# Dilated attention of a decoder layer on one Trainium2 core: both heads of a pair step together, and outputs are normalised behind the values

## What is computed

```python
h = _rms_norm(x, attn_norm_g)
z = h @ w_in                                   # q, k, v (8 heads of 64) and a, g (512 each)
q, k = _rms_norm(q, q_norm_g), _rms_norm(k, k_norm_g)
# attention: a query at t reads t, t-d, ..., t-window for (window, d) in (128,1), (512,4), (2048,16);
# the three softmaxes are combined with weights proportional to their denominators
attn, k_state, v_state = attend(q, k, v)
u = a * jax.nn.sigmoid(g)
c = silu(layer_norm(causal_depthwise(u, conv_w, conv_b)))     # 31 taps
x = x + concat([attn, c]) @ w_out
h = _rms_norm(x, ffn_norm_g)
x = x + (silu(h @ w_gate) * (h @ w_up)) @ w_down              # 2816 wide
```

## Time and profile before

| | us |
|---|---|
| Median of 3 runs | 1406.88 (1405.79 to 1413.41) |
| The profiled execution | 1401.69 |
| Its span | 1399.9 |
| Attention, first scores to first mean of the layer norm | 234.4 |
| Busy over the span: TensorE, VectorE, ScalarE, GpSimd | 1316.2, 785.7, 464.5, 540.8 |

### The profile page before, as it was taken

One profiled execution on the slowest core, in us unless ns is written; L12 is line 12 of the kernel. 1 busy time (PEld: TensorE's weight loads), 2 busy tenths in 40 slices (PEclk: granted clock), 3 DMA queues, 4 the chain that ended last, 5 costly groups with the idle time before them and its releaser, 6 DMA issues.

```text
span 1399.9 us, 22728 instructions
## 1 busy us (share of the span) xinstructions
PE 1316.2 (94%) x9073; PEld 1193.2 (85%) x9073; DVE 785.7 (56%) x1260; ACT 464.5 (33%) x868; POOL 540.8 (39%) x403
## 2 busy tenths in 40 slices
PE   6799999869889899997899999999999999999998
PEld 6799888736555558996899999999999999999998
DVE  5589999966556465769534343434434333434436
ACT  6211222136454453555432322223231313141311
POOL 0231453100000006264565556556464645464631
PEclk9899999969999899999899999999999999999999
DMA  6221322272525322100141424233241415050203
GB/s 208 65 65 38 113 88 97 82 250 91 183 67 206 129 102 77 35 1 1 61 163 55 166 76 136 106 106 136 76 166 46 167 45 186 26 196 16 91 31 129
DMA packets 54541, 142.68 MB, mean 102 GB/s; under 512 B 13728, under 2 KB 27040, under 8 KB 53856
## 3 DMA queue, kind: packets, MB, share of 16 engines
q1 hardware_dynamic: 48944, 107.28, 22.7%
q10 hardware_dynamic: 5504, 34.11, 7.2%
HBM read 129.68 MB, written 49.70 MB: 128 GB/s over the span
## 4 chain that ended last, share of the span: by engine, by line
PE 70%; DVE 15%; issue 4%; POOL 3%; ACT 2%; DMA 1%; SPq 0%; ACTq 0%; DVEq 0%; POOLq 0%
PE ps L1067 10%; PE ps L1070 10%; PE ps L375 10%; PE ps L1069 10%; PE ps L376 9%; PE ps L377 9%; DVE ps L1470 7%; PE ps L870 4%; PE ps L894 3%; PE ps L914 2%; POOL ring L698 1%; POOL ringf L706 1%; PE ps L926 1%; PE ps L883 1%; DVE tb L1611 1%
## 5 line engine op out<-in xcount | busy, mean ns | idle before, releaser
L1886 DVE TENSOR_TENSOR y<-ps,y 128x362 f32<-128x362 f32 (+1 forms) x264 | 141.4, 535 | 156.0 <-PE ps L377 156.0
L1067 PE MATMUL ps<-mh,ring 128*128 128x272 f32 x704 | 204.3, 290 | 2.7 <-issue 2.7
L1070 PE MATMUL ps<-mh,ring 128*128 128x272 f32 x704 | 204.5, 290 | 0.0
L1069 PE MATMUL ps<-ml,ring 128*128 128x272 f32 x704 | 204.1, 290 | 0.0
L698 POOL TENSOR_TENSOR ring<-fraw,ring 128x512 fp32r<-128x512 f32 x110 | 141.8, 1309 | 147.1 <-ACT ring L1270 89.6
L375 PE MATMUL ps<-ah,ring 128*128 128x362 f32 (+1 forms) x528 | 174.1, 330 | 6.6 <-issue 5.0
L376 PE MATMUL ps<-al,ring 128*128 128x362 f32 (+1 forms) x528 | 173.3, 328 | 0.0
L377 PE MATMUL ps<-ah,ring 128*128 128x362 f32 (+1 forms) x528 | 173.2, 328 | 0.0
L1470 DVE SCALAR_TENSOR_TENSOR ps<-uc,cws,ps 128x1024 f32<-128x1024 f32 x116 | 149.3, 1287 | 3.2
L706 POOL TENSOR_TENSOR ringf<-fraw 128x512 f32<-128x512 f32 x66 | 92.4, 1400 | 141.0 <-issue 73.6
L698 POOL TENSOR_TENSOR ring<-ringf,ring 128x512 fp32r<-128x512 f32 x88 | 118.5, 1362 | 61.4 <-ACT ring L1270 60.8
(11 more groups left out here) (198 smaller groups left out, 3224.2 us busy)
## 6 DMA issues: line engine op xcount, KB each, us to landing
fraw<-in_w_stream SPq DMA_DIRECT2D x66, 512.0 KB, 4.2
raw<-in_w_stream SPq DMA_DIRECT2D x28, 512.0 KB, 3.8
skt<-in_kT_c SPq DMA_DIRECT2D x32, 384.0 KB, 5.1
sv<-in_v_c SPq DMA_DIRECT2D x32, 384.0 KB, 5.2
qkv_scratch<-zo SPq DMA_DIRECT2D x24, 256.0 KB, 2.2
xr<-in_xT SPq DMA_DIRECT2D x8, 544.0 KB, 4.2
out_yT<-y SPq DMA_DIRECT2D x8, 544.0 KB, 2.7
raw<-qkv_scratch SPq DMA_DIRECT2D x8, 512.0 KB, 5.2
```

The source lines that it names most:

```text
L1067: pe.matmul(out, rhi(p)[:, col], rh[:, k, :], start=k == 0 and not onto, stop=False, skip_group_check=onto)
L1069: pe.matmul(out, rhi(p)[:, col], rl[:, k, :], start=False, stop=False, skip_group_check=onto)
L1070: last = pe.matmul(out, rlo(p)[:, col], rh[:, k, :], start=False, stop=k == KT // 2 - 1, skip_group_check=onto)
L1886: dve.tensor_tensor(y[:, oc, b0:b0 + bn], bank(4 + m % 4, bn), y[:, oc, b0:b0 + bn], ALU.add).then_inc(dn_y, 1)
```

## The change

Attention is written anew, everywhere else only names move.

- A pair has ten *steps* (`STEPS`): query blocks 0 to 3 (both heads), samples 0 to 3, blocks 4 to 7, samples 4 to 7. All 40 steps are written out.
- `scores` issues both heads' matmuls in turns, head 0 into banks 0 (and 1), head 1 into 2 (and 3); for blocks 1 and 3 into banks 1 and 3. Scores of the next step go first where the banks differ (`early`, steps 0 to 2), else between the turnings of the two heads.
- The scores come out negated (q's factor is negative, the mask too); VectorE takes the minimum, and exp runs with scale -1 and the minimum as bias. The negation L1615 is gone.
- `norm` is gone. `turn` waits for exp. Every four query blocks VectorE spreads the eight reciprocals of a head pair into `on` (128x512), TensorE transposes them, ScalarE copies them to `of`, VectorE multiplies the values' sums with `of`, then splits as before. Samples' sums are multiplied by the reciprocal before they are transposed, in place of a copy.
- `qt`, `kt`, `vn` have a second buffer (pairs in turns). The next q and k are transposed in steps 5, 6 and 7, `vn` is loaded a pair ahead, `vns` behind the last values.
- All copies of transposed probabilities are ScalarE's: in each step exp of both heads, then the copies of both heads, then those of q and k, then `of`.
- Masks are loaded before the weight pieces from 2 on. The residual's rows 0 to 3 (instead of 0 to 2) are loaded late, and wait for the last values.

```diff
-Y_LATE = 3
+Y_LATE = 4
 E1_ORDER = list(range(Y_LATE, KT)) + list(range(Y_LATE))
...
+STEPS = [("p", i) for i in range(4)] + [("s", 0)] + [("p", i) for i in range(4, 8)] + [("s", 1)]
+NST = len(STEPS)
+NG_A = NPAIR * NST
+UNIT = [0, 2, 4, 6, 8, 9, 11, 13, 15, 17, 18]
+NU = UNIT[NST]
+TURN_AT = {5: (0, 1), 6: (2, 3), 7: (4, 5)}
 QK_Q = 6
+OUT_OF = {3: 0, 4: 1, 8: 2, 9: 3}
+VECTOR_TURNS = ()
...
+def unit(g, h):
+    p, n = divmod(g, NST)
+    return p * NU + UNIT[n] + h
+def score_banks(n):
+    kind, i = STEPS[n]
+    if kind == "s":
+        return (0,)
+    return (0, 2) if i >= 4 or i % 2 == 0 else (1, 3)
+def banks_used(n):
+    w = 2 if blocks_of(n) > 4 else 1
+    return [b for b0 in score_banks(n) for b in range(b0, b0 + w)]
+def early(g):
+    return g + 1 < NG_A and not set(banks_used(g % NST)) & set(banks_used((g + 1) % NST))
...
+            for p in range(NPAIR):
+                if p + 1 < NPAIR:
+                    sp.wait_ge(d_tr, TURN["qk", p, 3] + 1)
+                    load_qk(cols_of(p + 1))
+                    sp.wait_ge(d_tr, TURN["qk", p, 5] + 1)
+                    load_qks(p + 1)
+                    if p >= 1:
+                        sp.wait_ge(d_pv, at_step(p - 1, 8) + 1)
+                    load_vn(p + 1)
+                else:
+                    sp.wait_ge(d_tr, TURN["qk", p, 3] + 1)
+                    for n in range(E0 + 4, E0 + 6):
+                        piece(n, n)
+                sp.wait_ge(d_s, at_step(p, 4) + 1)
+                load_sk(p * NB_S + 4)
+                sp.wait_ge(d_pv, at_step(p, 4) + 1)
+                load_sv(p * NB_S + 4)
+                if p + 1 < NPAIR:
+                    sp.wait_ge(d_s, at_step(p, 9) + 1)
+                    load_sk((p + 1) * NB_S)
+                    sp.wait_ge(d_pv, at_step(p, 9) + 1)
+                    load_vns(p + 1)
+                    load_sv((p + 1) * NB_S)
             sp.dma_start(y[:, Y_LATE:KT, :], xT[Y_LATE:KT].rearrange("k p n -> p k n")).then_inc(y_in[0], 16)
...
+            def scores(g):
+                p, n = divmod(g, NST)
+                kind, i = STEPS[n]
+                qt, kt_ = qts[p % 2], kts[p % 2]
+                if last_score_units(g):
+                    pe.wait_ge(d_tt, last_score_units(g))
+                if n == 0:
+                    turned_out(("qk", p, 3))
                 if kind == "p":
+                    nk = (i + 1) * P
+                    for c0 in range(0, nk, 512):
+                        cn = min(512, nk - c0)
+                        for h, b0 in enumerate(score_banks(n)):
+                            rows = slice(DH * h, DH * h + DH)
+                            last = pe.matmul(bank(b0 + c0 // 512, cn), qt[rows, i * P:(i + 1) * P],
+                                             kt_[rows, c0:c0 + cn], start=True, stop=True)
                 else:
+                    if i == 0:
+                        turned_out(("qk", p, 5))
...
+            def turn(g, h):
+                n = g % NST
+                pe.wait_ge(d_ex, unit(g, h) + 1)
+                for c in range(blocks_of(n)):
                     if c % 4 == 0:
+                        b = turn_bank(("t", g, h, c // 4))
+                    w = P if STEPS[n][0] == "p" or c < CKT else TS
+                    last = pe.transpose(bank(b, P, (c % 4) * P)[0:w, :],
+                                        tb[:, 2 * (g % 2) + h, c * P:c * P + w], ident[:])
...
+            def values(g):
+                p, n = divmod(g, NST)
+                kind, i = STEPS[n]
                 if kind == "p":
+                    if n == 0:
+                        pe.wait_ge(d_v[p % 2], 16 * (p // 2 + 1))
+                        if p:
+                            pe.wait_ge(d_of, 2 * p)
+                    if n == 5:
+                        pe.wait_ge(d_of, 2 * p + 1)
+                    for h in range(2):
+                        turned_out(("t", g, h, i // 4))
...
+            for g in range(NG_A):
+                p, n = divmod(g, NST)
+                if early(g):
+                    scores(g + 1)
+                if g:
+                    values(g - 1)
+                turn(g, 0)
+                if g + 1 < NG_A and not early(g):
+                    scores(g + 1)
+                if heads_of(n) == 2:
+                    turn(g, 1)
+                if p + 1 < NPAIR:
+                    for j in TURN_AT.get(n, ()):
+                        turn_qk(p + 1, j)
+                if g and (g - 1) % NST in OUT_OF:
+                    turn_outputs(g - 1)
+            values(NG_A - 1)
+            turn_outputs(NG_A - 1)
...
+            def exps(g, h):
+                n = g % NST
+                w = blocks_of(n) * P if STEPS[n][0] == "p" else SK
+                r = slice(UNIT[n] + h, UNIT[n] + h + 1)
+                v = tb[:, 2 * (g % 2) + h, 0:w]
+                act.wait_ge(d_tt, unit(g, h) + 1)
+                act.activation(v, v, ACT.Exp, scale=-1.0, bias=mns[:, r], accum_out=den[:, r]).then_inc(d_ex, 1)
...
+            for g in range(NG_A):
+                p, n = divmod(g, NST)
+                for h in range(heads_of(n)):
+                    exps(g, h)
+                for h in range(heads_of(n)):
+                    copy_probs(g, h)
+                if p + 1 < NPAIR:
+                    for j in TURN_AT.get(n, ()):
+                        copy_qk(p + 1, j)
+                if g and (g - 1) % NST in OUT_OF:
+                    copy_factors(g - 1)
             for b, (b0, w) in enumerate(LNB):
...
+            def mask_min(g, h):
+                p, n = divmod(g, NST)
+                kind, i = STEPS[n]
+                w = blocks_of(n) * P if kind == "p" else SK
+                mask = mkp[:, D - w:D] if kind == "p" else mks[:]
+                r = slice(UNIT[n] + h, UNIT[n] + h + 1)
+                if h == 0:
+                    dve.wait_ge(d_s, g + 1)
+                if g >= 2:
+                    before = g - 2
+                    hb = min(h, heads_of(before % NST) - 1)
+                    dve.wait_ge(d_tr, TURN["t", before, hb, (blocks_of(before % NST) - 1) // 4] + 1)
                 dve.sem_inc(own_wait, 1)
...
+            def normalise_outputs(g):
+                p, n = divmod(g, NST)
+                k = 4 * p + OUT_OF[n]
+                dve.wait_ge(d_ex, unit(g, heads_of(n) - 1) + 1)
+                if STEPS[n][0] == "p":
+                    r = slice(UNIT[n] - 6, UNIT[n] + 2)
+                    dve.reciprocal(rden[:, r], den[:, r]).then_inc(d_rc, 1)
+                    if k >= 2:
+                        dve.wait_ge(d_tr, TURN["out", at_step(*((p, 3) if n == 8 else (p - 1, 8)))] + 1)
+                    dve.wait_ge(d_rc, k + 1)
+                    dve.tensor_copy(on[:].rearrange("p i (h d) -> p (i h) d", d=DH),
+                                    rden[:, r].unsqueeze(2).broadcast_to([P, 8, DH])).then_inc(d_on, 1)
+                else:
...
+                    dve.tensor_scalar(so[:], bank(6, P), rden[:, r], None, ALU.mult).then_inc(d_on, 1)
+            def outputs(g):
+                p, n = divmod(g, NST)
+                k = 4 * p + OUT_OF[n]
+                kind, i = STEPS[n]
                 if kind == "p":
+                    dve.wait_ge(d_pv, g + 1)
+                    dve.wait_ge(d_ev, TURNED_OUT["out", g])
+                    dve.tensor_tensor(of[:], bank(7), of[:], ALU.mult).then_inc(d_of, 1)
+                    dve.wait_ge(d_of, 2 * p + (1 if n == 3 else 2))
+                    parts = [(slice(0, P), (i - 3) * P, 512, of[:])]
                 else:
...
+            for g in range(NG_A):
+                p, n = divmod(g, NST)
+                for h in range(heads_of(n)):
+                    mask_min(g, h)
+                if n == 0:
+                    fill_qb(p)
+                if g >= 2 and (g - 2) % NST in OUT_OF:
+                    outputs(g - 2)
+                if g and (g - 1) % NST in OUT_OF:
+                    normalise_outputs(g - 1)
+                for h in range(heads_of(n)):
+                    copy_probs(g, h)
+            outputs(NG_A - 2) if (NG_A - 2) % NST in OUT_OF else None
+            normalise_outputs(NG_A - 1)
+            outputs(NG_A - 1)
```

More of the change, by code:

```diff
@@ new lines, with by_vector, last_score_units @@
+TURNS = turn_order()
+TURN = {key: q for q, key in enumerate(TURNS)}
+def by_vector(key):
+    return key[0] == "out" and STEPS[key[1] % NST][0] == "s" or key[0] == "t" and blocks_of(key[1] % NST) > 4 and (
+        heads_of(key[1] % NST) == 2 and key[2] in VECTOR_TURNS)
+TURNED_OUT = {key: sum(by_vector(k) == by_vector(key) for k in TURNS[:q + 1]) for q, key in enumerate(TURNS)}
+def last_score_units(g):
+    mine = set(banks_used(g % NST))
+    last = 0
+    for e in range(g):
+        for h, b0 in enumerate(score_banks(e % NST)):
+            w = 2 if blocks_of(e % NST) > 4 else 1
+            if mine & set(range(b0, b0 + w)):
+                last = max(last, unit(e, h) + 1)
+    return last
@@ L843, in _, with turn_bank @@
             pe.wait_ge(v_z, NT)
```

(44 more changed lines are left out.)

442 lines of the change are left out of this document (177 added, 265 removed).

## The result

The changed kernel takes 1360.55 us (median of 4, 1357.43 to 1366.07) against 1406.97 us before (median of 4, in the same set of runs): a ratio of 0.967, 95% interval 0.962 to 0.971. In a later set, with six runs of the changed kernel and eleven of the kernel before, it was 0.966 (0.963 to 0.969). The forecast was 1370, the range 1352 to 1393. The profiled execution took 1357.43 us, its span is 1355.6. The single run of the kernel before beside the runs on loops, buffers, q and k and VectorE's copies took 1426.2 us at a mean granted clock of 0.95 (0.96 to 0.98 in all its other runs), and nothing is compared with it.

The account below looks back on a forecast made before the run. TensorE was taken to bound the kernel; pairs of 47.4 us plus the ends finish attention at 491.9 instead of 528.4, 36.5 us less, so 1365.2 profiled; the median 5.2 higher, forecast 1370, range 1352 to 1393.

Parts of the forecast that it names:

- the cheap end: Scores of both heads on two row groups: second head free, 9.3 us saved a pair; the dear end was no overlap.
- The cycles of the big steps: Steps 5 to 8 of a pair, followed through ScalarE's queue: 6.25, 6.75, 6.5 and 6.5, together 26.0 us.
- rival B: ScalarE's order costs more than followed: half a microsecond in each of ten steps, 20 us, hence 1390; chance 0.12.
- The step that was wrong: Exp releasing the turning directly, without reciprocal and product between (0.9 us at eight blocks), was counted as no gain.
- The second buffers: Doubled qt, kt, vn and earlier loads remove the 2.7 and 2.1 us waits and the drain at the change of pair.
- The ends: Start and end of attention: first exp at 293.7, last pair 45.0, surcharge, tail and clock fall; attention ends at 491.9 us.
- The start surcharge: Low clock of 0.50 for some 10 us at attention's start, less missing sample values: 2.5 us.
- The allowance of 1.2 a pair for hops: Rounded hops between engines in the steps of a pair, perhaps 1.2 us, chosen by the author.
- The tail: Behind the last exp cycle of attention: copies, sample values, product and one transpose, 2.2 us.
- Hidden things: Masks' issues in SyncE's queue, later y rows and loops written out were each claimed to cost or bring nothing.
- Rival C: Clock stays at 1.2 GHz in stretches of transposes in attention: slower, +62 us, 1432; chance 0.05.
- D: Cheaper rival: no clock fall and no lost hops in attention, 1360 or less, down to 1350; chance 0.2.

## Why the prediction was right

**Row groups.** Taken at the cheap end, and right: the second head is free. TensorE's pair is 41.4 us where 41.2 were worked out, and the scores of a pair, by the sum of their durations in the third pair, fell from 19.7 to 10.4 us: the 9.3 of the term. It is 7.7 of busy TensorE when taken out of the changed kernel, because one head's price held 0.2 us a step that the second does not pay. The column groups of rows 3 were the right neighbour, though no row of before showed this case: the cheap end was a choice. The Trainium skill (TensorEngine Tiling (Array Packing), Theoretical Speedup), up to 2 for a dimension of 64 or less, is borne out for rows: 1.89.

**The cycles of the big steps.** 26.0 us were worked out, 26.1 measured: 6.43, 6.77, 6.56 and 6.37 against 6.25, 6.75, 6.5 and 6.5 (turning of the first head starts at 359.53, 365.96, 372.73, 379.29 and 385.66). ScalarE's queue sets them as the working followed it: the last copy, then values beside exp. The small steps took 20.8 instead of 21.4. So a pair of 47.4 is 46.9, and rival B has no place: the 0.9 us waits for the last copy were in the sum.

**The step that was wrong: "in the big steps of before that was off the path, so I count no gain for it".** It holds for the big steps of the kernel before, where exps ran two units ahead of turning: in a pair TensorE waited for the division 0.29 us at a unit of four blocks and 0.77 us at one of samples, and at no unit of more blocks. In the new order exp is on the path, and a reciprocal and product behind it cost 28 us of waits, and up to 16 more with the clock. The total did not suffer, as the pair was worked out for the new order as it is; but the prediction gave the gain to row groups (35.6 of 36.5 us) and to the second buffers, and gave none to this part, while the run with the division in front of the turning (and VectorE doing both forms of it) shows nothing of the gain at the means.

**The second buffers.** "So the 2.7 and 2.1 us and the drain at the change of pair go": they went, but through the order. In the old order the earlier loads take the first and leave the second; in the new one the second `vn` is not needed. For `vn` the same gain was named under the wrong cause. What the second `qt` and `kt` bring, and so whether they or the order removed the drain at the change of pair, is open.

**The ends, term by term, from 491.9 to 484.1.** First exp at 294.2 instead of 293.7: +0.5. The start surcharge is 0.4 and not 2.5 (first exp to next pair's first exp 47.3 us): -2.1; the clock was low there only until 301, some 6 us and not 10, and why it cost so little was not tried. Three pairs of 46.9: -1.6, and the last taken as shorter by the same step: -0.5. The allowance of 1.2 a pair for hops, "my choice", was not needed: -4.8. No further fall of the clock in the pairs: -1.5. The tail was "copies, sample values, product, one transpose: 2.2"; what is left for it is 4.5, since the product waited for the split of the prompt's outputs (1.7 us of this came from GpSimd's cut beside it): +2.3. The sum is -7.7, with rounding the 7.8 measured. The forecast also added 5.2 us from the profiled execution to the median; here it was 3.1. So 1370 was 9.4 too high, most of it in two allowances, for hops (the way from one engine's end to the next one's start) and for the clock, that were chosen and not read from rows. The forecast of the tail named what follows on the path and not what stands ahead of it in VectorE's queue.

**Hidden things.** The masks' issues and `y` cost nothing: VectorE is through with the convolution at 293.3 us and the part behind the means takes 871.5 us in both profiles. The loops, put at nothing, brought between nothing and 1 us a pair.

**Rival C.** The clock stayed at 1.00 from 301 to 484 us, though transposes are 38% of TensorE's work in a pair, so C did not happen. The Trainium skill (TensorE: Matmul & The Clock Gate, Part 4) says that transposes do not count as busy. These 183 us do not decide that, since other matmuls stand between the transposes everywhere; they show only that this mix kept the full clock, and that C's step from the page to this kernel was wrong. D, "no clock fall and no lost hops", is what happened in the pairs, and the end gave part of it back.

## What to carry to other kernels

When float32 matmuls with a contraction of 64 can be spread over two row groups, count the second group as free (1.99 us for both heads against 1.98 for one), but work out the cycle of the new order across all queues first: a gain on TensorE reaches the end only if no other engine's hop stands in the same cycle, and two parts that each shorten one side of it can be worth little alone, as here with either of them taken out of the new order. Before a second buffer is added for a late load, see whether the new order leaves time for the load behind the last use of the old contents. At the end of a phase read which items stand in the queue ahead of the one that the next phase waits for.

## What the runs showed of the hardware that was not expected

**The clock fell while TensorE was busy.** With one row group it fell at 358 us, in the small steps at the second pair's start. From 350 us on TensorE had been busy but for 0.32 us at 356; the longest wait shortly before, 0.89 us at 348, stands in every pair; the changed kernel kept it through the same place (stretches of 5 us; first three rows one row group, last two the changed kernel):

```profile
350.00:355.00 5.00, 5.00 (x78) 3.73 (x77) 2.48 (x9) 2.37 (x8) 0.00 (x0) 1.00 0.46 170
355.00:360.00 5.00, 4.68 (x24) 2.43 (x25) 3.01 (x15) 2.62 (x9) 0.00 (x0) 0.82 0.66 188
360.00:365.00 5.00, 5.00 (x17) 2.50 (x16) 1.31 (x4) 0.98 (x5) 0.00 (x0) 0.50 1.02 309
...
350.00:355.00 5.00, 4.16 (x58) 2.65 (x53) 1.51 (x4) 3.05 (x8) 0.00 (x0) 1.00 1.09 282
355.00:360.00 5.00, 5.00 (x80) 3.62 (x80) 2.53 (x6) 3.11 (x8) 0.00 (x0) 1.00 1.04 363
```

So a fall is not always behind an idle gap, as rows 5 and 6 had led me to read it. What brought it about is open; the next pair of the same kernel, with the same waits, ran at 1.00 throughout.

**GpSimd held VectorE's subtraction.** It took 2.36 us beside GpSimd's cut, in each of the seven profiles looked at in which the two stand side by side, and 0.69 in the two without. It ended 0.55 us after the cut of 1.89 us did (483.29 against 482.74): nearly the time of one undisturbed subtraction. GpSimd's next piece of work, from 482.82, overlaps it in the records, whose spans on GpSimd are rough. The Trainium skill (Trainium Architecture — The Big Picture, What this means for kernel authors) says that the two engines share ports under an exclusive lock and do not split them; the wait for the whole cut agrees, the overlap with the next does not quite.

**Reading SBUF.** The cast of 128x512 out of SBUF took 0.43 us, against 0.69 for the subtraction of the same width.
